# Even attention: ScalarE scales the second key group's probabilities; instructions reordered in the odd layer and at the start of the even layer

## The reference

```python
# even layer: eight "dsa" heads over the 256 keys with the highest index score ...
_, idx = lax.top_k(score, topk)
p = masked_softmax(s, valid[:, None])
...
# ... and eight heads in two key groups with three kinds of keys, mixed by gates
return gq[..., 1:2] * o_s + gq[..., 2:3] * o_w          # selected ("slc") and window ("win")
o = g[..., 0:1] * o_c + o_sw                             # compressed ("cmp")
# compressed keys and values
h = jax.nn.gelu(jnp.einsum('bnlgd,ldf->bngf', blk, w1.reshape(CMP_BLOCK, D, CMP_HIDDEN)))
return jnp.einsum('bngf,fd->bngd', h, w2)
# odd layer: difference of two softmaxes, then a norm over each head's row
a = p[:, :, 0] - lam_val * p[:, :, 1]
o = rms_norm(o, subln_g) * (1.0 - lambda_init)
```

## Time and profile before

| | us |
|---|---|
| median of three runs | 2169.43 |
| range of the runs | 2166.93 to 2170.12 |
| the profiled execution | 2167.3 |
| its span, first to last instruction | 2165.5 |
| TensorE busy | 2090.1 |
| VectorE busy | 1371.5 |
| ScalarE busy | 919.1 |
| GpSimd busy | 287.3 |
| mean granted TensorE clock | 0.991 of full speed |

### The profile page before, as it was taken

How to read it: one execution, slowest core, us unless ns; L and a number is a source line. 1 busy time by engine, 2 the same in 40 slices (tenths; PEclk the granted TensorE clock), 3 DMA queues, 4 the chain that set the end, 5 groups by cost and what they waited for, 6 DMA issues and landing times.

```text
span 2165.5 us, 27150 instructions
## 1 busy us (share of the span) xinstructions
PE 2090.1 (97%) x10753; PEld 1665.5 (77%) x10757; DVE 1371.5 (63%) x2004; ACT 919.1 (42%) x1494; POOL 287.3 (13%) x336
## 2 busy tenths in 40 slices
PE   8989899999999999899999999999999999999998
PEld 7765568888888867688888888666878768888887
DVE  5878745867844388757787554355645435768753
ACT  4235545554543244445445442244423224544542
POOL 3420100000000244100000003020335320000000
PEclk9999999999999999999999999999999999999999
DMA  8520103233223432123332324131121213233231
GB/s 209 146 67 25 30 25 113 78 117 117 78 98 101 112 88 64 49 88 105 110 98 99 106 87 115 59 93 40 59 59 40 98 59 108 99 115 97 98 100 75
DMA packets 167336, 190.71 MB, mean 88 GB/s; under 512 B 21669, under 2 KB 125402, under 8 KB 167210
## 3 DMA queue, kind: packets, MB, share of 16 engines
q1 hardware_dynamic: 160592, 173.93, 25.7%
q0 software_dynamic: 6288, 14.93, 2.8%
q10 hardware_dynamic: 330, 0.12, 0.0%
HBM read 177.68 MB, written 2.17 MB: 83 GB/s over the span
## 4 chain that ended last, share of the span: by engine, by line
PE 80%; DVE 13%; ACT 3%; issue 2%; DMA 1%; POOL 0%; ACTq 0%; POOLq 0%; DVEq 0%
PE banks L457 68%; PE banks L2856 3%; DVE wl L392 2%; ACT wh L388 1%; PE banks L2975 1%; PE banks L1596 1%; DVE big L1284 1%; DVE sm L1542 1%; PE banks L1632 1%; DVE t L1156 1%; DVE big L1585 1%; PE banks L1515 1%; DVE m L1282 1%; DVE big L1159 1%; PE banks L2625 1%
## 5 line engine op out<-in xcount | busy, mean ns | idle before, releaser
L457 PE MATMUL banks<-uTh,wh 128*128 128x512 f32 (+1 forms) x1424 | 551.8, 387 | 9.7 <-DVE wl L392 4.1
L457 PE MATMUL banks<-uTh,wl 128*128 128x512 f32 (+1 forms) x1424 | 540.0, 379 | 0.0
L457 PE MATMUL banks<-uTl,wh 128*128 128x512 f32 (+1 forms) x1424 | 539.5, 379 | 0.0
L457 PE MATMUL banks<-wh,hTr 128*128 128x512 f32 x1552 | 488.1, 392 | 0.3 <-DVE hTr L2164 0.3
L392 DVE TENSOR_TENSOR wl<-stg,wh 128x2048 fp32r<-128x2048 f32 x133 | 312.5, 2350 | 227.5 <-ACT wh L388 227.1
L457 PEld LDWEIGHTS banks<-wh,hTr 128*128 128x128 f32 x1552 | 292.1, 188 | 64.6 <-DVE wl L392 2.4
L388 ACT ACTIVATE wh<-stg 128x2048 fp32r<-128x2048 f32 x133 | 253.0, 1902 | 193.1 <-PE banks L457 174.0
L457 PEld LDWEIGHTS banks<-uTh,wh 128*128 128x128 f32 x1424 | 269.6, 189 | 60.7 <-DVE wl L392 4.5
L457 PEld LDWEIGHTS banks<-uTh,wl 128*128 128x128 f32 x1424 | 269.1, 189 | 51.5
L457 PEld LDWEIGHTS banks<-uTl,wh 128*128 128x128 f32 x1424 | 269.9, 190 | 47.3 <-issue 0.5
L457 PE MATMUL banks<-wl,hTr 128*128 128x512 f32 x776 | 302.6, 390 | 0.0
(11 more groups left out here) (370 smaller groups left out, 2806.1 us busy)
## 6 DMA issues: line engine op xcount, KB each, us to landing
stg<-mlp_w_up SPq DMA_DIRECT2D x32, 1024.0 KB, 5.4
stg<-mlp_w_down SPq DMA_DIRECT2D x26, 1024.0 KB, 5.1
stg<-w_in SPq DMA_DIRECT2D x20, 1024.0 KB, 5.3
stg<-w_up SPq DMA_DIRECT2D x16, 1024.0 KB, 5.4
stg<-w_down SPq DMA_DIRECT2D x13, 1024.0 KB, 5.1
stg<-odd_w_in SPq DMA_DIRECT2D x16, 512.0 KB, 4.7
t<-p POOLq DMA_DIRECT2D x124, 64.0 KB, 2.0
big<-mlp_w_down SPq DMA_DIRECT2D x6, 1024.0 KB, 7.4
```

The source lines that it names most:

```text
L457: t = pe.matmul(outp, x, y, start=(start and k == 0 and m == 0), stop=(stop and k == n - 1 and m == 2))
```

## The change

It has five parts.

- Even attention, scaling. VectorE scales only group 0 of a unit's probabilities. For slc and win it first multiplies group 1's reciprocal by its gate (a 128x1 product); a new `act_prob` then scales group 1 on ScalarE with it, at the end of ScalarE's step, behind the exponentials of the next unit. TensorE's flip waits for the new signal `a_prob` ahead of its second half. The "cmp" units stay as they were.
- Top-k. 23 rounds stand ahead of the even attention, where there were 31; in the attention they come in the steps n > 4 with n mod 9 not 1 or 2, where also 3 and 4 were left out.
- Start of the even layer. VectorE's low half of piece ("in", "qb2") comes after 4 rounds of the top-k, not after 13; its part of the gelu comes before the split of the piece behind ("w1", 1, 1); GpSimd's part of the gelu comes before its rotation of ER 0; and VectorE turns in ER 0 and 1 in steps 1 and 3 of the attention, no longer ahead of it and in step 0.
- Odd attention, VectorE: `dve_rows_scale` comes before the generator `dve_dr` is stepped, and `dve_dr` turns a rotation in one step later than before.
- Odd attention, GpSimd: the power comes before the generator is stepped.

```diff
         def dve_query_hook(dve, n):
-            split("dve", ("w1",) + AT_QUERY[n])
-            take_more((13, 5)[n])
+            if n == 0:
+                take_more(4)
+                split("dve", ("in", "qb2"), 0)
+                take_more(1)
+            else:
+                take_more(3)
...
             dve.reciprocal(m[:, 4:6], m[:, 2:4]).then_inc(*v_prob.next(("even", n, 0)))
             dve.wait_ge(*v_prob.now())
-            for g in range(2):
-                r = m[:, 4 + g:5 + g]
-                if kind == "dsa":
-                    t = dve.tensor_scalar(p[:, g, 0:w], p[:, g, 0:w], r, None, ALU.mult)
-                else:
-                    x = (g * 4 + j) * 3 + (1 if kind == "slc" else 2)
-                    t = dve.tensor_scalar(p[:, g, 0:w], p[:, g, 0:w], r, gate[:, i, x:x + 1], ALU.mult, ALU.mult)
-            t.then_inc(*v_prob.next(("even", n)))
+            if kind == "dsa":
+                dve.tensor_scalar(p[:, 0, 0:w], p[:, 0, 0:w], m[:, 4:5], None, ALU.mult).then_inc(*v_prob.next(("even", n)))
+                return
+            x = [(g * 4 + j) * 3 + (1 if kind == "slc" else 2) for g in range(2)]
+            dve.tensor_tensor(m[:, 6:7], m[:, 5:6], gate[:, i, x[1]:x[1] + 1], ALU.mult).then_inc(*v_prob.next(("even", n, 1)))
+            dve.tensor_scalar(p[:, 0, 0:w], p[:, 0, 0:w], m[:, 4:5], gate[:, i, x[0]:x[0] + 1], ALU.mult, ALU.mult).then_inc(
+                *v_prob.next(("even", n)))
+
+        def act_prob(act, n):
+            kind, j, i = UNITS[n]
+            if kind == "cmp":
+                return
+            m, p, w = small[n % 16], PX[n % 4][:, 1, 0:width(n)], width(n)
+            act.wait_ge(*v_prob.at(("even", n, 0 if kind == "dsa" else 1)))
+            act.activation(p, p, ACT.Copy, scale=m[:, 5:6] if kind == "dsa" else m[:, 6:7]).then_inc(*a_prob.next(("even", n)))
...
             for g in range(2):
+                if g and UNITS[n][0] != "cmp":
+                    pe.wait_ge(*a_prob.at(("even", n)))
                 for k in range(width(n) // 128):
...
+        ER_DONE = {1: 0, 3: 1, **{n: m for n, (m, x) in ER_AT.items() if x == 2 and m >= 2}}
...
                     act_exp(act, n - 1)
+                if 0 <= n - 2 < N_UNITS:
+                    act_prob(act, n - 2)
...
-                if n in ER_AT and ER_AT[n][1] == 2:
-                    dve_er(dve, ER_AT[n][0])
+                if n in ER_DONE:
+                    dve_er(dve, ER_DONE[n])
...
-                if n > 4 and n % 9 not in (1, 2, 3, 4):
+                if n > 4 and n % 9 not in (1, 2):
                     take_more(1)
...
             for m in range(len(DR) + 2):
                 if m < len(DR) and DR[m][2] == 0:
                     split("dve", DR[m][1])
+                yield
                 if m >= 2:
                     dve_turned_in(dve, m - 2, DR[m - 2][0], DR[m - 2][3])
-                yield
                 yield
...
+                if rows_at(n, SCALE) is not None:
+                    dve_rows_scale(dve, rows_at(n, SCALE))
                 next(dr, None)
                 if rows_at(n, TOTAL) is not None:
                     dve_rows_total(dve, rows_at(n, TOTAL))
-                if rows_at(n, SCALE) is not None:
-                    dve_rows_scale(dve, rows_at(n, SCALE))
...
             run(dve_gate(dve), dve_rope(dve, r_query, dve_query_hook))
-            take_more(4)
-            dve_er(dve, 0)
+            take_more(6)
+            dve_gelu(dve)
             split("dve", ("w1", 1, 1))
-            dve_gelu(dve)
...
             run(pool_rope(pool, r_query))
+            run(pool_gelu(pool))
             pool_er(pool, 0)
-            run(pool_gelu(pool))
```

More of the change, by code:

```diff
@@ L213, in build @@
         a_hi, a_sq, a_part, a_keep, a_rope = [signal(n) for n in ("a_hi", "a_sq", "a_part", "a_keep", "a_rope")]
-        a_up, a_exp, a_flip, a_misc, a_hg = [signal(n) for n in ("a_up", "a_exp", "a_flip", "a_misc", "a_hg")]
+        a_up, a_exp, a_prob, a_flip, a_misc, a_hg = [signal(n) for n in ("a_up", "a_exp", "a_prob", "a_flip", "a_misc", "a_hg")]
         v_lo, v_add, v_part, v_keep, v_rope = [signal(n) for n in ("v_lo", "v_add", "v_part", "v_keep", "v_rope")]
@@ L2242, in pool_diff @@
             for n in STEPS:
-                next(dr, None)
                 if rows_at(n, TOTAL) is not None:
                     pool_rows_total(pool, rows_at(n, TOTAL))
+                next(dr, None)
                 yield
```

## The result

The changed kernel takes 2159.24 us (median of 8 runs, 2156.69 to 2163.33) against 2169.45 for the kernel before (8 runs, 2164.95 to 2173.23) on the same chip: ratio 0.9957, 95% interval 0.9946 to 0.9969, about 10 us faster. The forecast was 2151 with a range from 2142 to 2162. So the sign and the range held, but the gain is little over half of the 18.1 us. No execution took the median itself: four lie from 2156.7 to 2157.1 us and four from 2161.4 to 2163.3. The profiled execution is the slowest of these, 2163.33 us, 4.0 less than the profiled one of before. Lines of the changed kernel are 4 to 16 higher than before, and those of the experiments up to 4 higher or lower than the changed kernel's.

A forecast was written before the change was run, and what follows sets the result against it. TensorE and VectorE were taken as near their limit together, with only TensorE's idle time and low clock to win. 12.6 (start) + 2.8 ((c), (d)) + 2.7 ((e)) = 18.1 us, giving 2151 us; range 2146 to 2157, with rivals 2142 to 2162.

The forecast's parts named there:

- (c): Even attention: VectorE scales one group and top-k rounds move in; 5.5 us gained, plus 1.0 of clock.
- (e): Odd attention: waits for the rows' scaling go, new waits for queries come, the clock regains 3.0 us; +2.7 us.
- rival 1: ScalarE becomes the pacer of the even attention; (c) and (d) give -5 us, 2159 us; chance 0.12.
- (a): Even layer's start: earlier split of qb2 ends its wait; first product on the compressed keys 7.0 us earlier.
- (b): Even attention's start: rotations go behind the maxima of units 0 and 2; 3.9 us, plus 1.7 of clock.
- The 1.7 us of clock: Even layer, 100 to 150 us: part of (b), low-clock time regained once the waits go, 1.7 us.
- (d): Even attention: second half of each flip waits for ScalarE's scaling; -3.7 us, 3.0 of it in dsa.
- the ring: Even attention: copy, two exponentials and scaling on ScalarE against TensorE's step; 0.75 us per dsa head, 0.7 in slc and win.
- 1.53 us in each of six heads: Odd attention, part of (e): new TensorE wait for the turned-in queries at a head's first scores; seventh head 2.9 us.
- (f): GpSimd's power ahead of its rotation: they stand in different steps, so its order stays; 0 us.
- rival 2: Odd attention: the late queries dominate, low clock follows each new wait, (e) is -6 us; 2160 us; chance 0.11.
- rival 4: Better case: (d) is 0 and the clock stays up in (e); 2142 us; chance 0.07.

The follow-up runs named there:

- e11: The kernel before with only the even layer's start and the top-k order changed; both groups scaled on VectorE, odd layer as before: 2155.69 us, ratio 0.9940.
- e3: The changed kernel with ScalarE's scaling in slc and win alone; VectorE scales both groups in the dsa units: 2154.44 us, ratio 0.9945.
- e2: The changed kernel with both groups scaled on VectorE again; start, top-k order and odd layer as changed: 2156.47 us, ratio 0.9951.
- e6: The changed kernel with ScalarE's scaling put ahead of the next unit's exponentials in the step: 2155.41 us, ratio 0.9941.
- e9: The changed kernel with GpSimd's product by the cosine in the odd layer's rotations cut to one column of 512: 2153.99 us, ratio 0.9935.
- e4: The changed kernel with the odd layer's turning in one step earlier again, the rows' scaling kept ahead: 2152.66 us, ratio 0.9934.
- e7: The changed kernel with ScalarE's scaling followed by a second pass over the same columns with factor 1: 2175.15 us, ratio 1.0031.
- e10: The changed kernel with VectorE scaling both groups in dsa and, in the odd layer, only the keys' turning in one step late: 2149.57 us, ratio 0.9915.
- e12: As e10, and in the slc and win units ScalarE's scaling stands ahead of the exponentials, as in e6: 2148.70 us, ratio 0.9909.
- e1: The changed kernel with its odd-layer edits undone (rows' scaling, turning in and power where they stood): 2157.89 us, ratio 0.9959.

## Why the prediction was right, and where it was wrong

The sign and the range were right, and the start of the even layer made them so. The scaling and the odd layer, (c) to (e), were to give 5.5 us together and by e11 gave nothing or less. That the time still lies inside the range is owed to the size of the start and to a range 20 us wide. That it meets rival 1's 2159 is luck: the rival took all of the shortfall from the even attention.

(a) Held. 7.9 us by the first product on the compressed keys, forecast 7.0. The split came at 97.71, but took 3.92 us, with GpSimd's product beside it from 98.17; it was early enough for that not to matter.

(b) Held in its mechanism. No wait for a DMA stands ahead of unit 0's maximum, and its flip came at 129.90. (The forecast's 129.6 is 129.8 by its own terms, 7.0 and 3.9.) From the first product on the compressed keys to this flip the changed kernel gained 2.9 us for 3.9, since the wait of 1.65 us for L1456 took the clock down (0.62 from 125.0 to 129.5 us); e3, in whose trace the clock stayed up there, gained 3.8. The 1.7 us of clock lie behind the flip, where the kernel before ran at 0.51: the changed kernel gained 1.1 there, e2 1.5. In all the start gave 11.9 us for 12.6.

(c) and (d), the step that failed. For slc and win the sum had 5.5 us from the halved scaling, 1.0 from the clock and -0.7 for ScalarE's scaling: +5.8. The trace has +1.7, and 0.8 of these are there in e2 too. VectorE's waits did go, by 9.2 us counted from starts, more than the 5.5 taken. What was mis-sized is the ring: I let it bind only at the last flips of a run of nine, 0.7 us, and it binds in 23 flips and takes 9.7 us. Moving the scaling gave 0.5 to 0.9. The dsa units came as computed: four waits of up to 0.70 us where 0.75 was forecast, -3.2 for -3.0. On ScalarE's multiplications the rule of the Trainium skill ("ScalarE: Activation LUTs", Rules for kernel authors) agrees with the outcome in dsa (e3) and isn't borne out either way in slc and win. The scaling of 512 columns took 0.72 us on ScalarE for 0.54 on VectorE, but what cost time in dsa was its place in ScalarE's step: e6, with the same work in another order, loses 0.9 us there for 3.2.

(e) Held in its mechanism, wrong in size: +2.7 forecast, -0.9 measured. The waits were to cost 0.3 us and the clock to give 3.0. Between the two instructions of the table TensorE's idle time grew by 5.9 us and its busy time fell by 5.1, at a mean clock of 0.97 for 0.96. Five of the "1.53 us in each of six heads" were 1.6 to 2.3 and the seventh 2.3 for 2.9, but the first was 3.60 us, and the clock stayed low for the products behind it:

```profile
768.85 0.78 PE L457 MATMUL banks<-uTh,wh 128*128 128x512 f32 x1
769.43 0.63 PE L457 MATMUL banks<-uTl,wh 128*128 128x512 f32 x1
...
773.69 0.59 PE L457 MATMUL banks<-uTh,wl 128*128 128x512 f32 x1
```

Twelve products at the low level, about 0.2 us each, 2.4. Also the wait of 2.0 us for the rows' rest, which was to go, became two, 4.1 us. By e9 the excess of the first wait is GpSimd's product beside VectorE's scaling; the turned-in step of head 0 stands behind it.

(f) Held: nothing came of it.

Of the rivals, 1 comes nearer for (c) and (d) than the forecast: it had -5 us, the forecast +2.8, and from 148.82 us to the last dsa unit the two gave -1.5. Its mechanism is half right: ScalarE was waited for in 23 of the 32 slc and win flips, but in slc and win that cost no more than VectorE's waits before. For the odd layer rival 2 had -6 us; -0.9 is nearer to the forecast's 2.7. The low clock didn't follow each wait: in heads 2 to 5 it is 1.00 behind waits of 1.6 to 2.3 us. Some sums of the prediction are off by a little: 24 products of 0.23 us are 5.5 and not 5.6 us, and rival 4's terms give 2143 and not 2142. Nothing hangs on them.

The profiled execution lost another 5.5 us where nothing was changed. 1.6 are behind the last dsa unit: the same wait of 2.01 us as before, and products at 0.63 us behind it, which there were not before; eight of the thirteen profiled executions have them and five (e3, e4, e7, e10, e12) don't. 0.8 come near 1610 us and are clock: 0.83 from 1600 to 1620 us, where the kernel before had 0.91 in the same place. 2.9 are in the second model's attention. VectorE there, and GpSimd:

```profile
1446.91 2.74 DVE L2597 TENSOR_SCALAR p<-p,sm 128x528 f32<-128x528 f32 x2
```

```profile
1447.29 2.07 POOL L2470 TENSOR_TENSOR big<-big,k_c_win 128x896 f32<-128x896 f32 x1 [3.46 <-DMA big<-pad]
```

In the kernel before the same pair of VectorE's instructions took 0.90 us and ended 0.03 us before GpSimd's product started. In e4 the product starts in the middle of the pair's second one and nothing is late. 1.9 us are lost at the pair, and 1.0 in a stretch of low clock right behind it. Three of thirteen profiled executions have the long pair (the changed kernel, e1 and e2), and the same three have that stretch. GpSimd waits there for a DMA, so a few tenths of a microsecond in its landing may decide over 2.9 us. This may have a part in the two groups of times of the changed kernel, of which the profiled one is in the upper. But the groups lie some 5 us apart, and what parts them isn't shown, as the other runs have no trace.

## What to carry to other kernels

Moving work to an idle engine pays only if its result isn't wanted in the same step: ask what stands before it in that engine's queue and who waits behind it, and work out the ring for the middle units too, not for the widest alone. Before delaying an instruction by a step, look who asks for its result in that step; here half of the delayed instructions were worth 6.7 us more than all of them. Where a wait goes, look for it on the other side of the same instruction before counting it as won: 9.2 us went ahead of the flips and 9.7 came inside them. Also undo the parts of a change that gains as a whole, one by one: here the start and the order of the rounds alone gained no less than all of it.

## What the runs showed of the hardware

Where one of VectorE's products or scalings from SBUF and one of GpSimd's products overlap by more than 0.2 us, one of the two is long. In the odd attention L2090 with 384 columns takes 0.48 us alone and 1.5 to 2.1 beside GpSimd's product of 1.3; the split takes 2.29 alone and, in the two kernels, 3.7 to 3.9. At 794.74 us it was the other way: GpSimd's product took 3.39 us beside a split of 2.50. The maxima, which read PSUM, took 0.69 us (512 columns) beside it as alone. e9 shows that it is GpSimd's product, and no load or DMA, that makes VectorE's instructions long.

The Trainium skill ("SBUF — State Buffer", SBUF: two separate sides) says that the two engines share a pair of ports as an exclusive lock, which whoever starts first holds for the whole instruction. The lengths agree with that. Who will be held up can't be read from the recorded starts: GpSimd's product started 0.24 us behind a split at 794.50, and was long; it started 0.23 us behind the one at 815.07, took its usual 1.28, and the split took 3.68.

After equal waits the clock was not always equal. Behind the wait of 2.01 us at the last dsa unit it fell in some executions and not in others. In e9, where the waits at the heads' starts are all alike (1.61 to 1.75 us), it fell behind the first and not behind the next four; windows of heads 1 and 2, length, busy us per engine, clock:

```profile
764.10:785.70 21.60, 20.03 (x102) 15.13 (x102) 13.08 (x26) 9.53 (x24) 4.51 (x10) 0.92 0.29 73
```

```profile
785.80:806.20 20.40, 18.82 (x106) 14.37 (x106) 14.92 (x30) 10.12 (x25) 7.87 (x11) 1.00 0.31 79
```

So a clock term taken from the length of a wait alone, as in the forecast's (b) and (e), is a guess. A stretch that came or stayed away was worth 0.9 us here (unit 0's flip, changed against e3) to 2.4 us (head 1).
